# Two serial stretches re-ordered and all gathered v rows summed on VectorE, in a two-block transformer kernel

## The reference, cut to what matters

```python
# cross attention (4 heads, 256 wide), T = 512 queries, 256 keys
w = softmax(q @ k.T)                       # per head; then w @ v

# sliding-window attention and GLA read slices of one projection
aq, ak, av, gq, gk, gv, gg, glr = split(h @ w_in)

# PEER: u, v are [16384, 1024]; expert, gates are [tokens, 8 * 16]
ub  = take(u, expert)                      # 128 rows of 1024 for each token
hid = gelu(einsum('tkd,td->tk', ub, x)) * gates
vb  = take(v, expert)
y   = einsum('tk,tkd->td', hid, vb)
x   = x + gate2 * y
out = rms_norm(x, final_norm_w)            # [1, 512, 1024]
```

## Time and profile before

| what | value |
|---|---|
| median of 3 runs | 3118.39 us (3099.41 to 3122.19) |
| the profiled execution | 3108.99 us, its span 3107.2 us |
| mean granted TensorE clock | 0.952 |
| busy: PE, DVE, POOL, ACT | 2808.6 (90%), 1653.8 (53%), 1350.9 (43%), 918.9 (30%) us |
| dense u products, L1690 | 444.1 us busy, 128 steps |
| dense v products, L1730 | 441.4 us busy, 128 steps |
| DVE's u rows, L2364 | 256 of 1225 ns |
| DVE's v rows, L2378 | 214 recorded, of 1292 ns |
| chain that ended last | PE 63%, DVE 14%, DMA 13%, ACT 4%, issue 4%, POOL 3% |

### The profile page before, as it was taken

One profiled execution on the slowest core, in us unless ns is written; L12 is line 12 of the kernel. 1 busy time (PEld: TensorE's weight loads), 2 busy tenths in 40 slices (PEclk: granted clock), 3 DMA queues, 4 the chain that ended last, 5 costly groups with the idle time before them and its releaser, 6 DMA issues.

```text
span 3107.2 us, 32966 instructions
## 1 busy us (share of the span) xinstructions
PE 2808.6 (90%) x12354; PEld 2121.4 (68%) x12354; DVE 1653.8 (53%) x3186; ACT 918.9 (30%) x1695; POOL 1350.9 (43%) x979
## 2 busy tenths in 40 slices
PE   8989997889999889999896789999999999999824
PEld 6856886768788678888775668888887744444301
DVE  1032144743236243530305637999956999666675
ACT  3264244422434333222325232111113920000001
POOL 4422434734546224344342232444445944544574
PEclk9999998989999999999997899999999999999967
DMA  4300322003224126653230032999999289999997
GB/s 152 101 7 14 95 82 87 2 28 98 92 102 136 54 79 193 213 187 101 83 95 28 6 117 85 373 389 388 384 365 364 82 323 380 390 409 409 409 340 279
DMA packets 216991, 584.40 MB, mean 188 GB/s; under 512 B 23921, under 2 KB 48642, under 8 KB 216322
## 3 DMA queue, kind: packets, MB, share of 16 engines
q1 hardware_dynamic: 137312, 301.22, 28.0%
q0 software_dynamic: 74688, 271.61, 22.7%
q10 hardware_dynamic: 4834, 9.46, 0.9%
HBM read 574.88 MB, written 7.35 MB: 187 GB/s over the span
## 4 chain that ended last, share of the span: by engine, by line
PE 63%; DVE 14%; DMA 13%; ACT 4%; issue 4%; POOL 3%; SPq 0%; DVEq 0%; ACTq 0%; POOLq 0%
PE ps L1228 14%; PE ps L1230 13%; PE ps L1229 13%; PE ps L1690 10%; DMA rows<-in_v,expert 6%; DMA rows<-in_u,expert 6%; DVE ps L2378 3%; POOL rows L1147 3%; DVE rows L2364 1%; PE ps L1306 1%; PE ps L1194 1%; PE ps L1718 1%; PE ps L1319 1%; PE ps L1246 1%; PE ps L1244 1%
## 5 line engine op out<-in xcount | busy, mean ns | idle before, releaser
L1052 POOL TENSOR_TENSOR wlo<-wraw,whi 128x1024 fp32r<-128x1024 f32 x258 | 624.8, 2430 | 957.6 <-ACT whi L569 957.5
L569 ACT ACTIVATE whi<-wraw 128x1024 fp32r<-128x1024 f32 x258 | 270.7, 1058 | 821.1 <-PE ps L1230 714.6
L1228 PE MATMUL ps<-hhi,whi 128*128 128x512 f32 x1096 | 432.3, 394 | 17.9 <-DVE hlo L1855 6.0
L1730 PE MATMUL ps<-stream,hg 128*128 128x512 f32 x1024 | 441.4, 594 | 7.0 <-DMA stream<-in_v 7.0
L1690 PE MATMUL ps<-haff,stream 128*128 128x256 f32 x2048 | 444.1, 380 | 2.2 <-ACT stg L959 2.2
L1229 PE MATMUL ps<-hlo,whi 128*128 128x512 f32 x1096 | 429.6, 392 | 0.0
L1230 PE MATMUL ps<-hhi,wlo 128*128 128x512 f32 x1096 | 429.5, 392 | 0.0
L1690 PEld LDWEIGHTS ps<-haff,stream 128*128 128x128 f32 x2048 | 390.1, 191 | 55.7 <-ACT stg L959 2.4
L1147 POOL DMA_INDIRECT rows<-in_u,expert x256 | 263.1, 1028 | 273.9 <-DVE hid L2364 152.0
L1730 PEld LDWEIGHTS ps<-stream,hg 128*128 128x128 f32 x1024 | 194.9, 191 | 253.3 <-issue 244.8
L2364 DVE CUSTOM_DVE_ANT_0 rows<-rows,h_s 128x1024 f32<-128x1024 f32 x256 | 311.7, 1225 | 101.4 <-DMA rows<-in_u,expert 97.5
(11 more groups left out here) (455 smaller groups left out, 4342.0 us busy)
## 6 DMA issues: line engine op xcount, KB each, us to landing
stream<-in_ut SPq DMA_DIRECT2D x128, 512.0 KB, 6.7
stream<-in_v SPq DMA_DIRECT2D x128, 512.0 KB, 6.8
wraw<-in_w_in SPq DMA_DIRECT2D x96, 512.0 KB, 3.6
wraw<-in_w_ada SPq DMA_DIRECT2D x48, 512.0 KB, 4.0
wraw<-in_w_gu SPq DMA_DIRECT2D x88, 256.0 KB, 3.7
wraw<-in_w_down SPq DMA_DIRECT2D x22, 512.0 KB, 3.6
wraw<-in_w_br_ssm SPq DMA_DIRECT2D x16, 512.0 KB, 3.5
wraw<-in_w_xkv SPq DMA_DIRECT2D x16, 512.0 KB, 3.6
```

Of the source, the lines that this page charges most:

```text
L569: act.activation(whi[:, n % WSLOTS, 0:kn, :], wraw[:, n % WSLOTS, 0:kn, :], ACT.Copy).then_inc(w_hi, 1)
L1052: pool.tensor_tensor(wlo[:, n % WSLOTS, 0:kn, :], wraw[:, n % WSLOTS, 0:kn, :], whi[:, n % WSLOTS, 0:kn, :].bitcast(F32), ALU.subtract).th ...
L1228: pe.matmul(dst, lh, rh, start=k == 0, stop=False)
L1730: ins = pe.matmul(ps[:, 2 * i + half, :], hg[:, n, P * i:P * i + P], stream[j][:, 4 * half:4 * half + 4, :], start=n == 0, stop=n == NKEYS ...
```

## The change

It has three parts, with nothing shared between them.

First, cross attention: `px` has four buffers and the maxima, signs, sums and reciprocals have a slot of 16 columns each (`xa_m`, `xa_n`, `xa_s`, `xa_r`), so nothing waits for a buffer of two tiles before. ACT copies a tile's transposes one tile later (`xa_copy`), behind the exponentials of the next tile. DVE's order is written out: maxima run up to two tiles ahead of weights and copies.

Second, DVE empties its two jobs of group `in4` before block 0 of the sliding window, not between blocks 0 and 1.

Third, PE sums no rows, and nothing makes diagonals. DVE sums all 256 v rows, on `row_sums(0)` and `row_sums(1)` in turn, and waits for the row before the last. POOL's `first_hot` writes its matrix into `hot1` with two buffers like the others, and issues no gather inside the mixing stage. Head 4's `row_gelu` stands behind dense step 110 instead of 107, head 5's behind the mixing stage instead of step 118. The score loads of `top_keys` 12 and 13 (`load_scores` 10 and 11) are issued one block earlier. `sum_rows` joins a tile's two accumulators, `add_rows` scales and adds it; both tiles' `add_rows`, the dense tiles' additions, one root over four tiles and four scalings follow the last row, and tiles are stored in the order 0 to 3.

The functions that only the removed rows used (`row_wait`, `row_diags`, `row_half`, `hole_diagonal`, `own_sums`, `add_dense`, `add_tile`, `root_begin`, `root_end`, `scaled_out`, `later_weights`, `between_rows`) are gone and stand above; the rest of the diff is this:

```diff
-GELU_AT = {21: 0, 40: 1, 66: 2, 91: 3, 107: 4, 118: 5}
-PE_HOLE = [(12, k) for k in range(TOPK)]
-PE_TAIL = [(b, k) for b in (28, 30, 31) for k in range(1, TOPK, 2)]
-PE_ROWS = PE_HOLE + PE_TAIL
-PE_BLOCKS = sorted({b for b, _ in PE_ROWS})
-DVE_ROWS = [(b, k) for b in range(len(BLOCKS)) for k in range(TOPK) if (b, k) not in PE_ROWS]
-DIAGS, POOL_HOTS = 4, 4
-ENDS = (0, 2, 3, 1)
+GELU_AT = {21: 0, 40: 1, 66: 2, 91: 3, 110: 4}
...
-        smx = stat[:, 64:72]
-        snm = stat[:, 72:80]
-        ssum = stat[:, 80:88]
+        xa_m, xa_n, xa_s, xa_r = (stat[:, 64 + 16 * n:80 + 16 * n] for n in range(4))
...
-        px = at("px", TT, 16, [P, 2, 4, MEM])
+        px = at("px", TT, 16, [P, NT, 4, MEM])
...
-        diag = at("diag", CONST, 2.5, [P, DIAGS, P])
-        hot_pool = at("hot_pool", CONST, 4.5, [P, POOL_HOTS, NKEYS])
...
+            def xa_copy(i):
+                act.wait_ge(s("ptr_ready"), 2 * i + 1)
+                act.activation(ptx[:, 0:4, P * i:P * i + P], b4(6), ACT.Copy).then_inc(s("pt_act"), 1)
+
             for i in range(NT):
                 act.wait_ge(s("xmax_ready"), i + 1)
-                if i >= 2:
-                    act.wait_ge(s("ptr_ready"), 2 * (i - 1))
                 for h in range(XA_HEADS):
-                    act.activation(px[:, i % 2, h, :], ps[:, 2 * (i % 3) + h // 2, 256 * (h % 2):256 * (h % 2) + 256], ACT.Exp,
-                                   bias=snm[:, 4 * (i % 2) + h:4 * (i % 2) + h + 1], accum_out=ssum[:, 4 * (i % 2) + h:4 * (i % 2) + h + 1]).then_inc(s("pexp_ready"), 1)
-                act.wait_ge(s("ptr_ready"), 2 * i + 1)
-                act.activation(ptx[:, 0:4, P * i:P * i + P], b4(6), ACT.Copy).then_inc(s("pt_act"), 1)
+                    act.activation(px[:, i, h, :], ps[:, 2 * (i % 3) + h // 2, 256 * (h % 2):256 * (h % 2) + 256], ACT.Exp,
+                                   bias=xa_n[:, 4 * i + h:4 * i + h + 1], accum_out=xa_s[:, 4 * i + h:4 * i + h + 1]).then_inc(s("pexp_ready"), 1)
+                if i:
+                    xa_copy(i - 1)
+            xa_copy(NT - 1)
...
-                row_wait(act, block_of("u", t, h), TOPK - 1)
+                act.wait_ge(row_used, TOPK * (block_of("u", t, h) + 1))
...
-                if n == NKEYS - 2 and PE_HOLE:
-                    row_diags(PE_HOLE[:DIAGS])
...
-            for h in range(PEER_HEADS - 1):
+            for h in range(PEER_HEADS):
                 row_gelu(1, h)
-            if PE_TAIL:
-                row_diags(PE_TAIL[:8])
-                tile_squares((0, 1, 2))
-                row_diags(PE_TAIL[8:16])
-            row_gelu(1, PEER_HEADS - 1)
-            if not PE_TAIL:
-                tile_squares((0, 1, 2, 3))
-            tile_root((0, 1, 2))
-            row_diags(PE_TAIL[16:])
-            if PE_TAIL:
-                tile_squares((3,))
-            tile_root((3,))
+            for i, t in enumerate((0, 2, 3, 1)):
+                act.wait_ge(x_ready, NT * 4 + i + 1)
+                act.activation(yout[:, t, :], xf[:, t, :], ACT.Square, accum_out=ssq[:, t:t + 1]).then_inc(usq_ready, 1)
+            act.wait_ge(usq_ready, part_count(4, 0, NT - 1))
+            root(meps)
...
             def first_hot(b):
 
-                if b >= POOL_HOTS:
-                    pool.wait_ge(s("mix_mm"), b - POOL_HOTS + 1)
+                if b >= 2:
+                    pool.wait_ge(s("mix_mm"), b - 1)
                 for m in HOT_POOL:
                     c = 4 * b + m
-                    ins = pool.tensor_scalar(hot_pool[:, b % POOL_HOTS, :], cst[:, C_IOTA:C_IOTA + P], slot_t[:, 1, c:c + 1], slot_t[:, 0, c:c + 1], ALU.is_equal, ALU.mult)
+                    ins = pool.tensor_scalar(hot1[:, b % 2, m, :], cst[:, C_IOTA:C_IOTA + P], slot_t[:, 1, c:c + 1], slot_t[:, 0, c:c + 1], ALU.is_equal, ALU.mult)
                 ins.then_inc(s("hot1_pool"), 1)
 
-            gathered = [0]
-
-            def gather_next():
-
-                b, k = divmod(gathered[0], TOPK)
-                if k == 0 and BLOCKS[b][0] == "u":
-                    pool.wait_ge(s("head_done"), top_done(*BLOCKS[b][1:]))
-                gathered[0] += 1
-                gather(b, k)
-
-            late = 1 if PE_HOLE else 0
             load_scores(0)
             load_scores(1)
-            for b in range(len(BLOCKS)):
+            for b, (kind, t, h) in enumerate(BLOCKS):
+                if kind == "u":
+                    pool.wait_ge(s("head_done"), top_done(t, h))
                 for k in range(TOPK):
                     if k == RING and b == MIX_AFTER + 1:
                         pool.wait_ge(s("slots_ready"), 1)
                         for m in range(ND // 4):
                             first_hot(m)
-                            if PE_HOLE and m % 4 == 0 and m > 4:
-                                gather_next()
                         load_scores(8)
                         load_scores(9)
-                    if k == RING:
-                        if b - 1 in TOP_AFTER and TOP_AFTER[b - 1] < 10:
-                            q = TOP_AFTER[b - 1] - 4 + 2
-                            if q < 8:
-                                load_scores(q)
-                        if b - 1 - late in (12, 13):
-                            load_scores(TOP_AFTER[b - 1 - late] - 2)
-                    if TOPK * b + k == gathered[0]:
-                        gather_next()
+                    if k == TOPK // 2 and b - 1 in TOP_AFTER and TOP_AFTER[b - 1] - 2 < 12:
+                        q = TOP_AFTER[b - 1] - 4 + 2
+                        if q not in (8, 9) and q < 12:
+                            load_scores(q)
+                    gather(b, k)
...
-                    ins = transpose(ps[:, 6 + n // 4, P * (n % 4):P * (n % 4) + P], px[:, i % 2, n // 2, P * (n % 2):P * (n % 2) + P])
+                    ins = transpose(ps[:, 6 + n // 4, P * (n % 4):P * (n % 4) + P], px[:, i, n // 2, P * (n % 2):P * (n % 2) + P])
...
-                    first = hot_pool[:, b % POOL_HOTS, :] if m in HOT_POOL else hot1[:, b % 2, m, :]
-                    ins = pe.matmul(ps[:, b % 4, P * m:P * m + P], hot2[:, b % 2, m, :], first, start=True, stop=True)
+                    ins = pe.matmul(ps[:, b % 4, P * m:P * m + P], hot2[:, b % 2, m, :], hot1[:, b % 2, m, :], start=True, stop=True)
                 ins.then_inc(s("mix_mm"), 1)
-                if PE_HOLE and b % 4 == 1:
-                    row_half(b // 4, 0)
-                if PE_HOLE and b % 4 == 3:
-                    row_half(b // 4, 1).then_inc(s("pe_row_used"), 1)
...
-            for r in range(len(PE_HOLE), len(PE_ROWS)):
-                row_half(r, 0)
-                row_half(r, 1).then_inc(s("pe_row_used"), 1)
...
+            def xa_weights(i):
+                p4 = slice(4 * i, 4 * i + 4)
                 v.wait_ge(s("pexp_ready"), 4 * (i + 1))
-                link(v.reciprocal(srec[:, p4], ssum[:, p4]))
-                v.tensor_tensor(px[:, i % 2], px[:, i % 2], srec[:, p4].unsqueeze(2).to_broadcast([P, XA_HEADS, MEM]), ALU.mult).then_inc(s("px_ready"), 1)
+                link(v.reciprocal(xa_r[:, p4], xa_s[:, p4]))
+                v.tensor_tensor(px[:, i], px[:, i], xa_r[:, p4].unsqueeze(2).to_broadcast([P, XA_HEADS, MEM]), ALU.mult).then_inc(s("px_ready"), 1)
+
+            def xa_copy(i):
                 v.wait_ge(s("ptr_ready"), 2 * i + 2)
                 v.tensor_copy(ptx[:, 4:8, P * i:P * i + P], b4(7)).then_inc(s("pt_dve"), 1)
+
+            xa_max(0)
+            xa_max(1)
+            xa_weights(0)
+            xa_max(2)
+            xa_weights(1)
+            xa_copy(0)
+            xa_max(3)
+            xa_weights(2)
+            xa_copy(1)
+            xa_weights(3)
+            xa_copy(2)
+            xa_copy(3)
...
             sw_max(0)
             sw_max(1)
+            group(G["in4"], (2, 3), to_tokens(gv_s, 0))
             for b in range(NT):
-                if b == 1:
-                    group(G["in4"], (2, 3), to_tokens(gv_s, 0))
...
+                b, k = divmod(rows_done[0], TOPK)
                 rows_done[0] += 1
                 kind, t, h = BLOCKS[b]
+                c = slice(TOPK * h, TOPK * h + TOPK)
                 n = TOPK * h + k
                 j, count = row_count(b, k)
                 if kind == "u":
                     v.wait_ge(row_landed[j], 16 * count)
                     v.tensor_tensor_reduce(rows[j][:], rows[j][:], h2_s[:, t, :], 1.0, 0.0, ALU.mult, ALU.add, hid[:, n:n + 1]).then_inc(row_used, 1)
                     return
-                if k == 0 and b in PE_BLOCKS:
-                    if PE_TAIL and b == PE_TAIL[0][0]:
-                        head_weights(t, h).then_inc(s("wrow_ready"), 1)
-                    v.wait_ge(s("wrow_ready"), PE_BLOCKS.index(b) + 1)
-                elif k == 0:
-                    link(head_weights(t, h))
+                if k == 0:
+                    v.wait_ge(s("row_gelu"), PEER_HEADS * t + h + 1)
+                    link(v.reciprocal(grec[:, h:h + 1], gsum[:, h:h + 1]))
```

(31 more changed lines are left out.)

## The result

The changed kernel took 3143.57 us (3137.95 to 3147.85, 4 runs) against 3113.35 us for the kernel before in the same comparison: a ratio of 1.0106, 95% interval 1.0084 to 1.0129. Forecast was slightly faster.

What follows compares the result with a forecast made beforehand. TensorE bounds up to 1942 us, then PE with the gathered-row ring, which sets the end. Terms: -16.3 before dense v ends, +9.9 behind it, net -6.4: 3112 us from a median of 3118.39; range 3090 to 3145.

Steps and rivals of the forecast that it cites:

- Cross attention: One buffer per tile and new program orders let the output products start earlier: gain 5.1 us, between 3 and 7.
- Value group: Sliding-window part: copies moved ahead shorten PE's 14.72 us stand before the third block's scores: gain 5.4 us, between 3 and 8.
- Into the mixing stage: End of dense u stage: without diagonals the first mixing product starts at about 2391.3 instead of 2394.15 us: -2.8.
- I cost it at nothing: Dense u stage: DVE's stand of about 8 us for head 4's later GELU costs nothing, up to +4.
- the term of -2.8: Dense u stage to first mixing product: ACT no longer held by the removed diagonals, 2.8 us sooner.
- Mixing stage: Between dense u and dense v: 98 us instead of 101.3, ACT late next, -3.0; bounds -5 and +6.
- rival B: TensorE cools in the mixing stage without row products: at half clock 118 us, net +14, 3132 us; chance 0.08.
- Tail and end: Behind dense v: 112 rows in 148 us, bounds 143 and 162, then 24.6 us; +9.9 with the 0.7 before them.
- the row of 1.99 us an issue: Profile row used for the tail: POOL's issue takes 1.99 instead of 0.94 us beside back-to-back u products.
- Rival A: Tail: POOL paces the ring, issuing at 2.29 us, so the tail takes 162: net +7.6, 3126 us; chance 0.20.
- The end: Behind the last row: additions, root, scalings and store now follow it, 24.6 us against 12.0.
- A and B together: Slow tail plus cooled TensorE in the mixing stage: would pass +31 us; slower by that much had chance 0.13.

Runs made afterwards that it cites:

- h3_two_late: Changed kernel with v rows summed on one accumulator up to the mixing stage, two behind it: 3102.22 us, ratio 0.9974 to the kernel before (chip 4).
- h2_gelu_early: Changed kernel with GELUs of heads 2, 3 and 4 behind dense steps 60, 80 and 100: 3113.12 us, ratio 0.9999 to the kernel before (chip 4).
- j2_before_two: Kernel before with v rows of blocks 2 to 10 summed on two accumulators in turn: 3150.80 us, ratio 1.0117 to the kernel before (chip 5).

## Why the prediction was wrong

**Front.** Cross attention: forecast 5.1, measured 5.06, with the output products starting as replayed. Value group: forecast 5.4, measured 4.1 in the recorded profile and 9 in most others. The mechanism was right, the size too low outside the recorded profile; the bound of 8 was too narrow.

**Into the mixing stage: the step that failed.** "I cost it at nothing" was written of the stands in the dense u stage, because a longer one of 13.48 us was in the trace and harmless. That row was read with the old pace. The text had DVE alternate its sums in the tail and drew the speed of 1.2 us a row there; it also said that DVE "catches up at 1.2" behind the stand, and didn't ask what else 1.2 does. In the kernel before the ring is emptied at 1.39, each gather waits for a sum, and eight gathers go out 1.39 apart. In the changed one nothing holds POOL, and they go out at 1.25, which is 419 GB/s asked by the rows alone of a DMA that gives 410, for 12 to 16 rows in a row beside a dense stage. (That 410 is the line that matters isn't shown: no pace between 1.25 and 1.39 was run.) On chips 1 and 3 that is harmless, and the forecast holds: the term of -2.8 came out as -2.9 (451.21 to 448.31). On chips 2, 4 and 5, and in the recorded run, the engines' signals come up to 19.5 us late from there on, and the term is +33.8 in the recorded run (+17 to +37 in the others) instead. h3_two_late, h2_gelu_early and j2_before_two show the cause in the program from both sides.

**Mixing stage.** Forecast 98 us, measured 96.8 to 97.8 in all traces of the changed kernel and its versions. PE stayed fast enough (a step in 1.49, a granted clock of 0.98), so rival B didn't come about.

**Tail and end.** 112 rows were left over, as forecast. They took 150.3 us in the recorded profile with 5.4 us of a late signal in them, 141.4 us on chip 3; forecast was 148. A v block of 16 sums takes 20.1 us and a u block, with POOL ahead, 20.3: the 21.5 per u block, taken between the row of 1.99 us an issue and DMA's pace, was too high on a chip without late signals. The page "SBUF — State Buffer" of the Trainium skill, section Who interferes with whom, gave 145 for the tail by its rule; 141.4 lies below both numbers, and below the forecast's own lower bound of 143: DVE, with landed rows waiting in the ring, took rows a little faster than the 1.28 us at which DMA brings them. Issues of 1.99 us did come back beside back-to-back u products (four in one late block of the recorded run, none on chip 3), so the row stands against the rule as well; it cost nothing there because the ring was ahead. It takes products without any gap: those four issues ran beside products 1.14 us apart, while issues beside products 1.28 us apart took 0.97 to 0.98 (chip 3). Rival A (162) didn't come about. The end: forecast 24.6, measured 24.73.

**Rivals.** None of them was this one. The text also says that A and B together, or A with a mixing stage at its upper bound, would pass +31; by its own terms they give +27.6 (-6.4 + 14 + 20) and +13.6 (-6.4 + 14 + 6). Rival A had POOL as too slow; what happened is that POOL wasn't held back at all. Without late signals the kernel does what was forecast, with a gain of 12 us instead of 6 (chip 3). The recorded 3143.57 us lies just inside the range, at its far end, by luck: for a reason that no case gave.

**What stays open.** Shown is that a long burst of gathers starts the loss, that it takes the pace and a stand with a full ring, and that it happened on three chips of five. Each chip was used once, so the chip can't be told from the loading of that time. What holds a signal back isn't shown. The records fit signals that reach the waiting engine late: PE's records go on, and DVE waits 5.42 us for its own instruction. But ends of matmuls are modelled, so PE's later steps may have been held themselves. One rival stands untested. Every execution on record has a span and a granted clock, so the profiler watched it, and where signals are late its landing records are missing by the thousand. The recording may have a part in the delay, and no run shows this kernel without it. The kernel before has no trace from chips 2, 4 and 5; that it loses nothing there rests on its times (3109 to 3113 us).

## What to carry to other kernels

A consumer that is slower than the transfers it drains is a throttle: before making it faster, look for every place where it meets a full ring, not only for the stretch that the speed is meant for, and ask what the producer's queue does when nothing holds it. A row that shows a stall to be harmless shows it for the pace at which it was recovered, and no other. And when a loss starts before anything that differs between two kernels has run, repeat both on the same chip before believing either.

## What the runs showed of the hardware

- With 12 to 16 gathers issued 1.25 us apart (419 GB/s asked for, 410 given) beside a dense stage, three of five chips brought engines' signals 1.6 to 19.5 us late; two chips never did. Eight such gathers in a row made one signal 1.5 to 2.3 us late on the same three chips and cost nothing. The kernel before took 3109 to 3113 us on all five, so the median of an unchanged kernel doesn't tell these chips apart.
- The traces of these three chips lack 1807 to 2614 of 18,688 landing records, the others 14 or 15.
- On the chips with late signals the tail has a delay of 3.8 to 5.4 us in the changed kernel's versions, with PE and the stream idle.
- The changed kernel's median differed by 36 us between chips 3 and 2 (3100.42 and 3136.45), nine times the spread of the kernel before's medians.
